# Reordering decode's second round, a layer norm's square root and a small V product in a hybrid decoder step

## The reference

```python
h = rms_norm(x, g_pre)
z = h @ w_in                      # q | k | v | attn gate | u | v_s | sgu gate, 3072 columns
att = attend(q, k, v)             # block-sparse (MoBA) attention; decode reads 8 pages of K and V per sequence
u, v = gelu(u), group_layer_norm(gelu(v_s))
gm = u * (tril(W_s[g]) v + b[g])  # within chunks of 128 positions
mix = concatenate([att * silu(gate_a), gm * silu(gate_g)])
y = x + rms_norm(mix @ w_out, g_post)
```

## Time and profile before

| | |
|---|---|
| median of 3 runs | 279.13 us (278.95 to 279.42) |
| the profiled execution | 279.68 us, its span 278.0 us |
| PE busy | 268.8 us, 97% |
| DVE, ACT, POOL busy | 188.3, 169.2 and 85.0 us |
| granted TensorE clock, mean | 0.997 |
| DMA | 43.39 MB, mean 156 GB/s |

### The profile page before, as it was taken

The page is one execution under the profiler, slowest core; times in us unless marked ns, Lnnn a source line. Parts: engine busy times, 40 slices in busy tenths (PEclk is TensorE's granted clock), DMA queues, the critical chain, the costliest instruction groups (busy, mean ns, idle before and its releaser), DMA issues.

```text
span 278.0 us, 6103 instructions
## 1 busy us (share of the span) xinstructions
PE 268.8 (97%) x2115; PEld 236.0 (85%) x2115; DVE 188.3 (68%) x485; ACT 169.2 (61%) x387; POOL 85.0 (31%) x98
## 2 busy tenths in 40 slices
PE   7999999999999999999998999999999999999992
PEld 2799998998997887998776999998998976768892
DVE  4695886599844545946347877877867894917772
ACT  5784569532693323178997687797786653627621
POOL 4557704310302032242042875443350410000000
PEclk9999999999999999999999999999999999999998
DMA  7999995469899969504563118004018304040053
GB/s 240 327 260 218 201 263 114 145 197 269 226 318 266 289 197 303 186 0 154 152 193 121 40 38 255 12 4 148 2 35 309 133 1 151 2 151 0 19 187 117
DMA packets 31026, 43.39 MB, mean 156 GB/s; under 512 B 3043, under 2 KB 23523, under 8 KB 30996
## 3 DMA queue, kind: packets, MB, share of 16 engines
q1 hardware_dynamic: 27266, 29.76, 38.1%
q0 software_dynamic: 3728, 13.24, 15.7%
q10 hardware_dynamic: 2, 0.00, 0.0%
HBM read 39.59 MB, written 3.41 MB: 155 GB/s over the span
## 4 chain that ended last, share of the span: by engine, by line
PE 69%; ACT 17%; DVE 9%; issue 3%; DVEq 0%; POOL 0%; ACTq 0%; POOLq 0%
PE Z L1486 10%; PE Z L1491 9%; PE Z L1487 9%; ACT probs L955 3%; PE T L1403 3%; PE S L1528 3%; PE O L1625 2%; ACT probs L964 2%; PE Z L1441 2%; PE S L1441 2%; PE S L1442 2%; PE Z L1443 2%; PE S L1443 2%; PE Z L1442 2%; ACT w_hi L811 2%
## 5 line engine op out<-in xcount | busy, mean ns | idle before, releaser
L1486 PE MATMUL Z<-act_hi,w_hi 128*128 128x288 f32 (+1 forms) x344 | 89.7, 294 | 0.4 <-ACT zvs L888 0.3
L1487 PE MATMUL Z<-act_lo,w_hi 128*128 128x288 f32 (+1 forms) x344 | 88.2, 288 | 0.0
L1486 PEld LDWEIGHTS Z<-act_hi,w_hi 128*128 128x128 f32 x344 | 64.8, 188 | 2.6 <-issue 1.6
L1487 PEld LDWEIGHTS Z<-act_lo,w_hi 128*128 128x128 f32 x344 | 64.8, 188 | 0.0
L704 POOL TENSOR_TENSOR w_lo<-w_raw,w_hi 128x1024 fp32r<-128x1024 f32 x16 | 38.3, 2395 | 57.5 <-ACT w_hi L811 57.5
L1491 PE MATMUL Z<-act_hi,w_lo 128*128 128x256 f32 (+1 forms) x336 | 48.9, 288 | 0.0
L1491 PEld LDWEIGHTS Z<-act_hi,w_lo 128*128 128x128 f32 x336 | 44.8, 188 | 0.0
L811 ACT ACTIVATE w_hi<-w_raw 128x1024 fp32r<-128x1024 f32 x32 | 33.5, 1050 | 15.0 <-DMA w_raw<-in_w_out 10.0
L1049 DVE TENSOR_TENSOR w_lo<-w_raw,w_hi 128x1024 fp32r<-128x1024 f32 x15 | 18.1, 1209 | 16.2 <-ACT w_hi L811 16.2
L955 ACT ACTIVATE probs<-probs,nmax 128x128 f32<-128x128 f32 (+3 forms) x32 | 17.7, 555 | 13.3 <-DVE nmax L1277 13.3
L1162 DVE STREAM_TRANSPOSE kT<-k_ring 128x1024 f32<-128x1024 f32 x16 | 19.8, 1236 | 0.4 <-PE S L1528 0.2
(11 more groups left out here) (271 smaller groups left out, 553.7 us busy)
## 6 DMA issues: line engine op xcount, KB each, us to landing
w_raw<-in_w_in POOLq DMA_DIRECT2D x10, 1024.0 KB, 7.1
k_ring<-in_cache_k SPq DMA_DIRECT2D x64, 128.0 KB, 4.5
v_ring<-in_cache_v SPq DMA_DIRECT2D x64, 128.0 KB, 3.3
w_raw<-in_w_out SPq DMA_DIRECT2D x8, 512.0 KB, 4.4
x_sb<-in_x_prompt SPq DMA_DIRECT2D x4, 512.0 KB, 5.5
w_raw<-in_w_in SPq DMA_DIRECT2D x4, 512.0 KB, 8.3
x_res<-in_x_prompt SPq DMA_DIRECT2D x4, 512.0 KB, 5.2
out<-y_sb SPq DMA_DIRECT2D x8, 256.0 KB, 2.1
```

The costliest lines, as they stand in the source:

```text
L1486: mm(out, wh[:, k, :], act_hi[:, k, cols], start=(k == 0), stop=False)
L1487: mm(out, wh[:, k, :], act_lo[:, k, cols], start=False, stop=False)
```

## The change

The list changes. Half 27 gets `DEX` 1 ahead of `VSN` 2. `DPT` 1 goes from half 30 to 29, the eight `DPV` of round 1 from halves 31 to 34 to 30 to 33, `DOD` 1 from 35 to 34, `DOT` 1 from 36 to 35. `VSN` 4 goes from half 29 to 30, behind the first two pages. `LN` goes from the front of half 32 to its end, behind `ATT` 0. `o_bank` follows `DOD` 1, so unit 3 gets bank 1. The product with the own V rows is issued as four column tiles of 32 over 128 contracted rows, of which all but the first 32 are zeros that POOL writes once at the start.

```diff
-    after(28, ("DEX", 1))
+    after(27, ("DEX", 1))
...
-    after(30, ("DPT", 1))
+    after(29, ("DPT", 1))
     for pg in range(8):
-        after(31 + pg // 2, ("DPV", 1, pg))
-    after(29, ("VSN", 4))
-    after(32, ("LN",))
+        after(30 + pg // 2, ("DPV", 1, pg))
+    after(30, ("VSN", 4))
...
-    after(35, ("DOD", 1))
-    after(36, ("DOT", 1))
+    after(34, ("DOD", 1))
+    after(35, ("DOT", 1))
...
+        if u == 2:
+            after(h, ("LN",))
...
-        kv_s = small("kv_s", [SMP, 514])
+        kv_s = small("kv_s", [P, 514])
-        p_ownT = small("p_ownT", [SMP, P])
+        p_ownT = small("p_ownT", [P, P])
...
+            nc.gpsimd.memset(p_ownT[:, :], 0.0)
+            nc.gpsimd.memset(kv_s[:, 0:512], 0.0)
...
-                        last = mm(O[1][:, 0:VW], p_ownT[:, :], kv_s[:, KVW:KVW + VW], start=False, stop=True, skip_group_check=True)
+                        for b in range(4):
+                            last = mm(O[1][32 * b:32 * b + 32, 0:VW], p_ownT[:, 32 * b:32 * b + 32], kv_s[:, KVW:KVW + VW],
+                                      start=False, stop=True, skip_group_check=True)
```

More of the change, by code:

```diff
@@ L757, in _ @@
                     else:
-                        pool.dma_start(kv_rows(k_prompt, k_sample, tt), kv_s[:, 0:KVW]).then_inc(stored_kvs, 16)
-                        pool.dma_start(kv_rows(v_prompt, v_sample, tt), kv_s[:, KVW:2 * KVW]).then_inc(stored_kvs, 16)
+                        pool.dma_start(kv_rows(k_prompt, k_sample, tt), kv_s[0:SMP, 0:KVW]).then_inc(stored_kvs, 16)
+                        pool.dma_start(kv_rows(v_prompt, v_sample, tt), kv_s[0:SMP, KVW:2 * KVW]).then_inc(stored_kvs, 16)
                 elif kind == "KTD":
@@ L910, in _ @@
                     else:
-                        take(n, kv_s[:, 0:512], T[n % 2][0:R, :])
+                        take(n, kv_s[0:SMP, 0:512], T[n % 2][0:R, :])
                     if tt < 4:
@@ L931, in _ @@
                     act.wait_ge(own_turned, r + 1)
-                    nc.scalar.activation(p_ownT[:, :].rearrange("p (b c q) -> p b c q", b=4, c=KVH),
+                    nc.scalar.activation(p_ownT[0:SMP, :].rearrange("p (b c q) -> p b c q", b=4, c=KVH),
                                          O[0][0:SMP, 256:256 + P].rearrange("p (c b q) -> p b c q", c=KVH, b=4), ACT.Copy).then_inc(p_own_turned, 1)
```

## The result

The changed kernel takes 280.9 us (280.55 to 281.26, 6 runs), against 279.13 for the kernel before (278.93 to 279.45, 5 runs): ratio 1.0063, 95% interval 1.0049 to 1.0077. It is slower by 1.8 us. One more run of the kernel before, at 283.53 us, and one of a kernel further down, at 285.42 us, lie more than 1.5% above the fastest of their kernel and are left out of the medians here. The forecast was slower by 0.7, with a range up to 280.8, so the direction was right and the size was not.

The account below looks back on a forecast made before the run. TensorE (PE), busy 97% of the span, bounds the kernel. PE's own 0.5 us delay and the ring's 0.85 meet at 192.99: 0.85 - 0.12 = 0.7 us later, so 279.8 us, range 278.3 to 280.8.

Parts of the forecast that it names:

- Exps at half 27: On ACT, ahead of VSN 2: Exps start at 118.9 us, 3.7 earlier; DOT 0's copies end only 0.6 earlier.
- Second round one half forward: At DPT 1, now in half 29: PE idles 1.9 us for DOT 0's copies, where it idled 0.53.
- VSN 4 behind it, Sqrt late: Unit 0's Exps start 2.65 us late, unit 2's at 143.1; PPV 1's wait vanishes, PPV 2 waits about 0.75.
- Tiles: Own V product takes 0.49 us instead of 0.63, 0.14 less twice; only the first counts, taken as 0.12.
- DOD 1 and DOT 1 one half earlier: On DVE: 0.6 and 0.85 us more ahead of the masks of units 4 and 5, the same less behind; cost 0.
- the ring: DVE mask, ACT Exp, normalisation, o_tmp, DVE sum, next mask: no visible slack, its 0.85 us delay meets PE at 192.99.
- third sign of being wrong: PE's idle at PTR 10 (the prediction's name for PTR 11) as short as before.
- B: Unseen slack absorbs the delay of the ring between 164 and 193 us; PE's own delay stays: 279.5 us, chance 0.15.
- C: Faster: DOT 0's copies end by 124.6 us, not 126.45, so PE's wait at DPT 1 goes: 277.9 us, chance 0.2.
- D: On ACT: Tanh's table after late Sqrt lacks Exp, so unit 3's Exps need another load, 1.1 us: 281.0, chance 0.07.
- E: VSN 4's four handovers between DVE and ACT cost some 0.2 us each, 0.8 more: 280.6 us, chance 0.05.
- F: The own V product's four tiles don't overlap: 2.5 us instead of 0.49, 2.0 on the path: 281.8, chance 0.03.

Follow-up runs that it names:

- first experiment: The changed kernel with DOT 1 put back from half 35 to half 36, all else kept: 280.11 us.
- DOD and DOT early: The kernel before with Exps at half 27, Sqrt late and tiles, plus DOD 1 at half 34 and DOT 1 at 35: 277.29 us.
- ring delay run: The kernel before with Exps at half 27, Sqrt late and tiles, plus two unused DVE instructions ahead of unit 7's mask: 278.38 us.
- three of these edits: The kernel before with only Exps at half 27, Sqrt late and the tiles: 276.5 us, ratio 0.9897.
- Sqrt at half 33: The changed kernel with DOT 0 ahead of VSN 3, DOT 1 back in half 36, LN at the end of half 33, LNM 4 in half 34: 280.89 us.

## Why the prediction was right or wrong

By its own steps, in its order:

- **Exps at half 27.** Right: the Exps start at 118.43 (118.9 forecast, less the 0.28 by which this execution is early and the tiles' saving), VSN 3's square at 123.88 (124.3). DOT 0's copies end at 125.97 against 127.03, which is 0.6 earlier once these two are taken off, as forecast.
- **Second round one half forward.** Right: 1.81 us of wait where 1.9 was forecast, released by the copies. DOT 0 ahead of VSN 3 gives 1.77 back.
- **VSN 4 behind it, Sqrt late.** Right within some 0.5 us: unit 0's Exps at 134.57 (134.9), unit 2's at 142.64 (143.1), unit 3's at 149.33 (149.8), PPV 1 without a wait, PPV 2 with 0.82 (0.75). Half 35 was forecast 0.5 late, without the tiles' 0.12; it is 0.38.
- **Tiles.** Size near: 0.19 a round, not 0.14. Of it 0.12 was booked, and the tiles alone give 0.10 on the stretch.
- **DOD 1 and DOT 1 one half earlier.** This is the step that failed. It costed them at zero, as DVE work that comes back one half later. I had counted them as work on DVE only, and had followed the bank order only for DPT 1. But DOT 1 is a use of the two T banks. Ahead of PTR 4 it makes the second half of PTR 4 the use two after DOT 1, so PE waits for copies that stand behind LNM 0: 1.22 us, worth 0.81 of time (first experiment), or 0.8 to 0.9 where nothing else is late (DOD and DOT early). Without DOT 1's move the changed kernel is at 280.11, 0.3 from the 279.8 on record, and its stretch is +0.67 where 0.7 was summed. Its two terms, PE's 0.38 and the ring's 0.66, came nearly as summed, so the rest of the sum is no luck, except for the place where they meet (next point).
- **The ring carries its delay to PE.** Right in that nothing is absorbed, by the ring delay run, and wrong in the place. The prediction lets ring and PE run apart until they meet at 192.99. In the changed kernel PE's wait at PTR 4 passes into the ring at once (DVE idles for PE at 165.22, and unit 6's mask is 1.46 us late, not 0.85), and PE is as late at half 37 as at the end. Its wait at PTR 11 is 0.32 against 0.35, which is the third sign of being wrong that the prediction names.
- **Rivals.** B is out by the ring delay run. C (no wait at DPT 1) did not come, but the condition it named, copies that VSN 3's sum does not hold, takes that wait away with one line moved; the time is then 279.04, or 278.33 with DOT 1 back, against C's 277.9. D is out: one load ahead of Tanh, at 147.55, also serves the Exp at 149.33. The Trainium skill (ScalarE activation tables: per-element evaluation and per-set limits, Table sets in the compiler and the runtime) says that loads are placed greedily by the longest run, and the trace agrees with it here. D's time was 280.9 by its own terms (279.8 + 1.1, not 281.0); that this is the measured time is chance. E did not come: unit 0's Exps start at 134.57, or 134.85 with the 0.28 added back, no later than the 134.9 that has none of its handovers. F is out: the tiles overlap.

The range failed with the step: 280.8 at its upper end against 280.9. Its upper end came from E, a doubt about handovers, and no rival had the bank order in it.

## What to carry to other kernels

When a step moves in a list that also numbers the uses of rotating buffers, recount who waits for whose buffer for every use behind it, not only for the step that moves. And when an engine has to read out a buffer that another engine waits for, let it do so before it starts on anything for which it waits itself: one line of order was worth 1.8 us here. Then try the parts of a change one at a time: three of these edits give 1.0%, and the round's forward move takes that back and 0.6% more.

## What the runs showed of the hardware

A DVE instruction that reads and writes SBUF was held up twice while GpSimd ran its multiply of LNM. In the ring delay run the two `tensor_scalar` of 256 fp32 columns took 1.61 us together, but not in equal parts: the first took 0.285 us and the second, the same instruction, 1.286. Rows of DVE and POOL there:

```profile
166.12 1.28 POOL L786 TENSOR_TENSOR vn<-vn,g_sgu_bc 128x512 f32<-128x512 f32 x1 [0.42 <-DVE vn L1270]
166.28 1.29 DVE L1281 TENSOR_SCALAR od<-od 128x256 f32<-128x256 f32 x1
```

The second started 0.16 us after POOL's instruction and ended 0.17 us after it. With Sqrt at half 33 LNM 0's multiply on DVE (L1270) started at 159.96, inside POOL's multiply from 159.49 to 160.79, and took 1.39 us where the other four took 0.68; it ended 0.56 us after POOL's. In both cases the end is about what one gets if the instruction does its work only when POOL's is over. It does not hold for every DVE instruction on SBUF: the reciprocal at 161.94 of the ring delay run kept its 0.16 us inside a POOL instruction that ran from 159.85 to 162.23. No run tests the cause by itself, and it was not in the prediction.
